# Eight sequences' states as moving operands in four column tiles, state eviction on VectorE, and a new order of steps, in a hybrid RWKV-7 / RetNet / MoE decoder step

## The reference, cut to what matters

```python
h = rmsnorm(x); proj = h @ w_in          # 2048 -> RWKV part (r,k,v,loras) and retention part (q,k,v,gate)
# RWKV-7, 16 heads x 64, per token, state S (value, key):
sa = S @ (-kk); S = S * w + outer(sa, b) + outer(v, k); y = S @ r
# then: group norm of y over the head, plus a bonus term, times a gate
# retention, 8 heads x 128, chunked, state R (key, value):
o = (q k^T * decay_in) v + (q R) * decay_q;   R = R * decay_c + (k * decay_k)^T v
x = x + concat(y_a, y_b) @ w_out
x = x + hier_moe(rmsnorm(x))             # top-1 of 4 groups, top-2 of 8 SwiGLU experts in it
y = rmsnorm(x)
```

## Time and profile before

| | us |
|---|---|
| median of 3 runs | 1986.51 (1985.43 to 1987.39) |
| the profiled execution's own time | 1987.42 |
| its span in the trace | 1985.3 |
| busy: TensorE (PE) | 1623.7, 82% |
| busy: VectorE (DVE) | 581.6, 29% |
| busy: ScalarE (ACT) | 288.5, 15% |
| busy: GpSimd (POOL) | 119.4, 6% |

### The profile page before, as it was taken

One profiled execution on the slowest core, in us unless ns is written; L12 is line 12 of the kernel. 1 busy time (PEld: TensorE's weight loads), 2 busy tenths in 40 slices (PEclk: granted clock), 3 DMA queues, 4 the chain that ended last, 5 costly groups with the idle time before them and its releaser, 6 DMA issues.

```text
span 1985.3 us, 25584 instructions
## 1 busy us (share of the span) xinstructions
PE 1623.7 (82%) x9086; PEld 1001.5 (50%) x9086; DVE 581.6 (29%) x1095; ACT 288.5 (15%) x577; POOL 119.4 (6%) x101
## 2 busy tenths in 40 slices
PE   8899999999999999999997668574867757676665
PEld 4677878686777777776774223132322312222111
DVE  6535454536354544431012111011110201111013
ACT  2222222222222222220012000000000000000002
POOL 1201111020202020200000000000000000000000
PEclk9999999999999999999999788787888878778778
DMA  7223222313223222217429999999999999999997
GB/s 287 81 79 115 78 99 74 111 67 108 84 77 112 77 102 87 95 63 281 181 117 385 428 427 428 428 429 429 428 428 428 428 429 428 429 429 428 428 409 261
DMA packets 71615, 510.34 MB, mean 257 GB/s; under 512 B 20464, under 2 KB 23664, under 8 KB 37648
## 3 DMA queue, kind: packets, MB, share of 16 engines
q1 hardware_dynamic: 71520, 509.60, 63.3%
q0 software_dynamic: 48, 0.12, 0.0%
HBM read 499.87 MB, written 9.82 MB: 257 GB/s over the span
## 4 chain that ended last, share of the span: by engine, by line
PE 54%; DMA 33%; DVE 7%; issue 2%; SPq 1%; ACT 1%; POOL 1%; DVEq 0%; POOLq 0%; ACTq 0%
DMA arena<-w_up 22%; PE ps_PJ L659 19%; DMA arena<-w_down 11%; PE ps_C L992 8%; DVE arena L1344 7%; PE ps_PJ L858 7%; PE ps_C L719 2%; PE ps_C L742 2%; SPq L515 1%; PE ps_C L1043 1%; PE ps_SB L1043 1%; PE ps_YB L1043 1%; PE ps_C L725 1%; PE ps_RT L824 1%; PE ps_SB L778 1%
## 5 line engine op out<-in xcount | busy, mean ns | idle before, releaser
L659 PE MATMUL ps_PJ<-arena 128*128 128x320 f32 x1792 | 536.6, 434 | 0.0
L992 PE MATMUL ps_C<-arena 128*32 128x512 f32 x2048 | 286.8, 723 | 189.6 <-DMA arena<-w_gate 113.1
L659 PEld LDWEIGHTS ps_PJ<-arena 128*128 128x128 f32 x1792 | 324.3, 191 | 112.3 <-issue 11.5
L992 PEld LDWEIGHTS ps_C<-arena 128*32 128x32 f32 x2048 | 79.5, 130 | 390.1 <-issue 387.7
L1344 DVE TENSOR_TENSOR arena<-arena,ps_PJ 128x512 f32<-128x512 f32 (+2 forms) x112 | 73.5, 657 | 614.9 <-PE ps_PJ L958 491.4
L1075 ACT ACTIVATE arena<-ps_C 128x512 f32<-128x512 f32 (+1 forms) x76 | 45.5, 598 | 1079.2 <-PE ps_C L992 581.4
L1344 DVE TENSOR_TENSOR arena<-arena 128x320 f32<-128x320 f32 (+13 forms) x254 | 143.8, 566 | 50.1 <-ACTq L379 25.8
L1832 POOL TENSOR_TENSOR arena<-arena 128x640 f32<-128x640 f32 (+2 forms) x80 | 113.6, 1420 | 734.2 <-ACTq L379 663.5
L858 PE MATMUL ps_PJ<-arena 128*128 128x320 f32 x512 | 144.1, 437 | 2.1 <-DVEq L379 2.1
L858 PEld LDWEIGHTS ps_PJ<-arena 128*128 128x128 f32 x512 | 96.5, 192 | 42.5 <-issue 6.2
L1075 ACT ACTIVATE arena<-arena 128x320 f32<-128x320 f32 (+11 forms) x149 | 79.6, 534 | 183.8 <-DVEq L379 60.6
(11 more groups left out here) (184 smaller groups left out, 1379.7 us busy)
## 6 DMA issues: line engine op xcount, KB each, us to landing
arena<-w_up SPq DMA_DIRECT2D x64, 2048.0 KB, 20.3
arena<-w_down SPq DMA_DIRECT2D x64, 2048.0 KB, 20.3
arena<-w_gate SPq DMA_DIRECT2D x60, 2048.0 KB, 21.0
arena<-win SPq DMA_DIRECT2D x59, 1024.0 KB, 4.8
arena<-w_out SPq DMA_DIRECT2D x16, 1024.0 KB, 5.8
arena<-w_gate SPq DMA_DIRECT2D x8, 1024.0 KB, 10.6
arena<-xT SPq DMA_DIRECT2D x8, 640.0 KB, 7.1
arena<-s_ret SPq DMA_DIRECT2D x8, 512.0 KB, 3.8
```

The costliest lines, as they stand in the source:

```text
L659: last = mm(pj(j)[:, 0:T], wt[j % NSLOT][:, kt, :], hT[:, kt, :], start=kt == 0, stop=kt == KT - 1)
L992: last = mm((GB, UB)[u][h * CAP:(h + 1) * CAP, :], xg[:, kt, h * CAP:(h + 1) * CAP], w[h][:, k, :], start=kt == 0, stop=kt == KT - 1)
```

## The change

Four things.

- In `sN` the product with the identity goes. VectorE takes the state out instead of ScalarE: `S = psum * w + Sw`, one fused operation, where `Sw` is the old state times the next decay, which VectorE makes right behind each eviction but the last (`s0` is a plain scaling).
- In `rs0` the operands change places. The 24 columns of a sequence are the stationary operand (`arx`, a copy with sequences outermost, made by ScalarE in step `pd`), the state is the moving one, 128 columns wide, and four sequences go to four column tiles of 32 output partitions, in two turns. The retention states that `oo` used one after another are done in the same way in `rs0` (`qdx` holds the 16-wide stationary operands, with zeros where another turn's sequence stands). The results lie as rows of sequences; they are put in order by products with 0/1 matrices: four products with 32-wide weights in `rs1`, one product in `oo`, two in `us`. `my` then copies all 320 columns of y at once.
- ScalarE's eviction of `rs0` is two copies (256 and 128 wide) for one of 192.
- The order: `ps` before `-s3`; `-mu` two fields later, behind `g4`; the five Gram products in four fields in a row, all of them in tile v; `lp ls` one field earlier; `v0 v1` ahead of `@v` on VectorE; `z1` stays in its field.

```diff
-    "r": "@k | -r3 | sq | -a3 ss | p1 | -s3 ps | | b1 b2a",
-    "v": "@r | | b2b | -my | -mu | g4 p2 | g0 | g1",
-    "q": "@v v0 g2 -va | g3 v1 | lp ls | | z1 | zs1 pd | | d1 ds1",
+    "r": "@k | -r3 | sq | -a3 ss | p1 | ps -s3 | | b1 b2a",
+    "v": "@r | | b2b | -my | g4 p2 | -mu g0 | g1 | g2 g3 v0",
+    "q": "v1 @v -va | lp ls | | | z1 | zs1 pd | | d1 ds1",
...
-                    if c > 0:
-                        mm(b[:, 0:P], ident, S, start=True, stop=False)
-                    mm(b[:, 0:P], tok[:, 1, c, :], SA, start=c == 0, stop=False)
+                    mm(b[:, 0:P], tok[:, 1, c, :], SA, start=True, stop=False)
...
-                    for i in range(NS):
-                        last = mm(ob[:, :, i * TS:(i + 1) * TS], S0[:, i, :], ar[:, :, i * TS:(i + 1) * TS], start=True, stop=True)
+                    for g in range(2):
+                        for c in range(4):
+                            mm(b[32 * c:32 * c + 24, g * P:(g + 1) * P], arx[:, 4 * g + c, :], S0[:, 4 * g + c, :], start=True, stop=True)
+                    for g in range(2):
+                        for c in range(4):
+                            last = mm(b[32 * c:32 * c + 16, 2 * P:3 * P], qdx[:, 4 * g + c, :], Rs0[:, 4 * g + c, :], start=g == 0, stop=g == 1)
...
-                    mm(b[:, 0:P], RTs[:, 0:P], ident, start=True, stop=False)
+                    for a in range(2):
+                        for g in range(2):
+                            mm(b[64 * a + 32 * g:64 * a + 32 * g + 32, 0:P], seq_heads[:, 32 * a:32 * a + 32], QA[:, g, :], start=True, stop=False)
...
+                    for g in range(2):
+                        mm(yb[:, 32 * g:32 * g + 32], QA[:, g, :], seq_rows[:, :, 16:24], start=False, stop=g == 1)
...
-                    for i in range(NS):
-                        cc = slice(TP + i * TS, TP + (i + 1) * TS)
-                        last = mm(b[:, cc], Rs0[:, i, :], qd[:, cc], start=False, stop=i == NS - 1)
-                    last.then_inc(full(s), 1)
+                    mm(b[:, TP:T], QO, seq_rows[:, :, 0:16].rearrange("p c (g t) -> p g c t", g=2), start=False, stop=True).then_inc(full(s), 1)
...
-                    A(S, bank(s)[:, 0:P], ACT.Copy, scale=wc(c)).then_inc(free(s), 1)
...
+                        TSC(S, bank(s)[:, 0:P], wc(0), None, ALU.mult).then_inc(free(s), 1)
+                    else:
+                        STT(S, bank(s)[:, 0:P], wc(c), Sw, ALU.mult, ALU.add).then_inc(free(s), 1)
+                    if c < NC - 1:
+                        TSC(Sw, S, wc(c + 1), None, ALU.mult)
```

More of the change, by code:

```diff
@@ L193, in build_program @@
         kdt, vrt = sb(384), sb(384)
+        qdx, seq_heads = qd[:, 0:P].rearrange("p (i n) -> p i n", i=NS), qd[:, TP:T]
+        arx = xm["k"][:, 0:24 * NS].rearrange("p (i n) -> p i n", i=NS)
         st = sb(T)
@@ L1140, in step @@
                     last.then_inc(done("vbd"), 1)
+                    wait_done(act, "bd", p)
+                    A(arx.rearrange("p i (a t) -> p a i t", a=3), AR[:, NC, :].rearrange("p (a i t) -> p a i t", a=3, i=NS), ACT.Copy).then_inc(done("arx"), 1)
                 elif s == "sq":
@@ L1183, in step @@
                     if s == "z5":
[L1184 to L1189, removed]
-                    A(S, bank(s)[:, 0:P], ACT.Copy, scale=wc(c)).then_inc(free(s), 1)
+                        A(wcs, e1[:, 0:TP].rearrange("p (c n) -> p c n", c=NC)[:, :, C - 1:C].rearrange("p c n -> p (c n)"), ACT.Copy).then_inc(done("wc"), 1)
                 elif s == "rs0":
                     wait_filled(act, s, p)
-                    A(RTs, bank(s)[:, 0:192], ACT.Copy).then_inc(free(s), 1)
+                    A(QA[:, :, :], bank(s)[:, 0:2 * P].rearrange("p (g n) -> p g n", g=2), ACT.Copy)
+                    A(QO, bank(s)[:, 2 * P:3 * P], ACT.Copy).then_inc(free(s), 1)
                 elif s == "va":
@@ L1422, in _ @@
                 shifted(lraw[j], lxm[j], lmu[0:m, j:j + 1], lmu[0:m, 3 + j:4 + j], m, sh_out[0:m, 24 + j, :], lora_xm)
+            for a in range(2):
+                CP(seq_heads[:, 32 * a:32 * a + 32].rearrange("p (c t) -> p c t", c=4), seq_rows[:, :, 8 * a:8 * a + 8])
             RED(sgn, rotm, AX_X, ALU.add)
@@ L1519, in step @@
                     CP(SA, bank(s)[:, 0:P]).then_inc(free(s), 1)
+                elif s in ("s0", "s1", "s2", "s3"):
+                    c = int(s[1])
+                    wait_filled(dve, s, p)
+                    if c == 0:
+                        wait_done(dve, "wc", p)
+                        if not first(p):
+                            dve.wait_ge(out_done["S"], 32 * p)
+                        TSC(S, bank(s)[:, 0:P], wc(0), None, ALU.mult).then_inc(free(s), 1)
[3 more added lines that the diff above has]
+                        TSC(Sw, S, wc(c + 1), None, ALU.mult)
                 elif s == "rs1":
@@ L1571, in step @@
                         dve.wait_ge(hc_in, 16 * (p + 1))
-                        TT(qd, x, dq, ALU.mult).then_inc(done("qrot"), 1)
+                        TT(qd[:, P:TP], x[:, P:TP], dq[:, P:TP], ALU.mult)
+                        for g in range(2):
+                            cc = slice(TP + 32 * g, TP + 32 * g + 32)
+                            last = TT(qdx[:, 4 * g:4 * g + 4, 8 * g:8 * g + 8], x[:, cc].rearrange("p (i t) -> p i t", i=4),
+                                      dq[:, cc].rearrange("p (i t) -> p i t", i=4), ALU.mult)
+                        last.then_inc(done("qrot"), 1)
                     else:
```

21 lines of the change are left out of this document (10 added, 11 removed), and 2 rows, old and new, of the table PLAN0.

## The result

The changed kernel takes 1958.28 us (median of 4 runs, 1957.59 to 1959.95) where the kernel before takes 1986.76 (median of 4, 1985.43 to 1987.39). The ratio is 0.9859, with a 95% interval of 0.9842 to 0.9876: 1.4% or 28.5 us less, a small gain, but clear of the noise. The profiled execution took 1959.95 (span 1958.2); that of before 1987.42 (span 1985.3).

What follows compares the result with a forecast made beforehand. TensorE bounds the mixing stage, busy 101.54 of 104.40 us a period. Loop 1.4 + 2.4 = 3.8 a pair, times 7, 26.6; first pair 1.2, tail +0.2: 27.6 less, 1986.51 to 1959 us, range 1953 to 1972.

Steps and rivals of the forecast that it cites:

- Work on TensorE: Per pair: 4.06 us of products removed, 2.68 added in `rs0`, `rs1`, `oo` and `us`; 1.4 us less.
- the round of four short passes: In `rs0`: four 128-column passes over four column tiles take 0.14 us a round, between 0.108 and 0.25.
- Rivals 1, 3 and 4: Column tiles dearer: loads not hidden, 1968 (13%); single file, 1982.5 (9%); single file with loads unhidden, 2017 (4%).
- rival 3: Short column-tile passes run in single file: 2.9 us a pair lost, 1982.5 us; chance 9%.
- rival 1: Weight loads in a column tile are not hidden: 0.25 us a round, 1968 us; chance 13%.
- The stretch from `s2` to `z1`: Holds all three TensorE waits; those at `lp` and `z1` go, `z1` starts 2.4 us earlier a pair.
- `ss` reaches VectorE 0.36 us earlier: In the `s2` to `z1` stretch: `a3`'s 0.29 wait goes, `s2` is 0.22 shorter; 575.54 instead of 575.90.
- Rival 2: The waits come back because VectorE sets the `s2` to `z1` stretch: 1.6 us a pair lost, 1970 us; chance 12%.
- rival 5: The gain is taken back by unseen waits: 1986 us; chance 3%.
- "I expect no clock effect there": In the mixing stage the granted clock is 1.00 (2.4 GHz), even where TensorE waits; no effect expected.
- First pair, tail, expert stage: Written-out first pair gains 1.2 us; behind the loop `s1` costs 0.65, `s2` and `s3` give 0.44: +0.2.
- "The expert stage keeps its length": Expert stage: DMA engines busy throughout at 428 GB/s, untouched by the change, so mixing-stage gains reach the end in full.

Runs made afterwards that it cites:

- one_tile: Changed kernel with all short products of `rs0` in the first column tile instead of four (output not the reference's): 1979.86 us.
- order_only: Kernel before with the new order table alone; state evictions on ScalarE and identity products stay: 1966.08 us, ratio 0.9896.
- evict_only: Kernel before with VectorE's fused state eviction alone, without identity products, old order but for `ps` ahead of `s3`: 1996.14 us, ratio 1.0039.
- tiles_only: Kernel before with the column tiles alone; old order, ScalarE evicts the states, identity products stay: 1973.58 us, ratio 0.9939.
- no_evict: Changed kernel with column tiles and new order, but states evicted on ScalarE and added by the identity as before: 1957.73 us, ratio 0.9854.
- same_tile_first: Changed kernel with loops exchanged for `rs0` and the retention states, so four passes in a row go to one tile: 1958.91 us, ratio 0.9847.
- g4_late: Changed kernel with one table row altered: `g4` and the `p2` behind it one part of a projection later: 1952.09 us, ratio 0.9823.
- s3_late_g4_late: Changed kernel with `g4` one part of a projection later and VectorE's eviction of `s3` behind the copy of y: 1947.6 us, ratio 0.9792.
- no_evict_g4_late: Changed kernel with the old state eviction on ScalarE and `g4` one part of a projection later: 1950.71 us, ratio 0.9813.
- old_order_filled: Changed kernel under the whole old order, with six 320-column matmuls added ahead of the wait at `mu`: 1987.28 us, ratio 1.0006.

## Why the prediction was right, and what in it was off

The forecast was 27.6 us less; the profiled execution gave 27.5 and the medians 28.5. The forecast 3.8 a pair is the measured 3.80. That agreement is partly luck: two terms were off in opposite directions.

1. **Work on TensorE**, forecast -1.4 a pair, measured about -1.6. The removed 4.06 is gone in full. Of the added 2.68, `rs1` came to 0.60 (0.35 for its tiles, 0.20 more on the product behind, 0.05 on the next projection) for 0.62, `us` to 0.42 for 0.43, `oo` to 0.22 for 0.17, but `rs0` to 1.20 (0.57 + 0.44 + 0.19) for 1.46. The term that was mis-sized is the round of four short passes: I took 0.14, between 0.108 and 0.25, and it is 0.11, the lower end. Entering the mode costs about 0.13 (0.57 less 0.44), leaving it 0.19 to 0.2.
2. **Rivals 1, 3 and 4** fall with that number. `one_tile` shows what rival 3 would have looked like: 3.6 us in `rs0`, which with its order and eviction still ends at 1980. The Trainium skill's rule that a weight load overlaps a running matmul only when the row group differs (TensorE: Matmul & The Clock Gate, The mechanism), on which rival 1 leant, does not describe these rows: four tiles with the same rows took 0.11 us a round, and even one tile 0.110 to 0.117 a pass. The kernel before could have said so: eight full-width passes of a projection, all with the same rows, take 2.16 us (the first line shown under 3), or 0.27 each, while their eight weight loads take 1.92 us beside them.
3. **The stretch from `s2` to `z1`**, forecast -2.4, measured about -2.2 (from `s2`'s first product to `z1`'s start it is 2.0 shorter, and `z1` itself, without a wait ahead, 0.27). The step that failed in it is that `ss` reaches VectorE 0.36 us earlier, for which the prediction names two terms, 0.29 and 0.22, and no sum. Measured from `s2`'s first product (568.88 before and 551.80 now, in the chains), k's shift did begin earlier, 2.44 us behind it for 3.23 (572.11), 0.8 instead of the 1.3 I wrote. But the wait at `a3` that this was to remove had cost next to nothing. It is a wait of the weight load alone, and the chain of before shows the products in a row across it:

```profile
572.82 2.16 PE ps_PJ L659 x8
574.98 0.27 PE ps_C L755 x2
```

   There `a3` takes 0.27 instead of its usual 0.22, so its wait was worth 0.05. The identity gave 0.22, and of that `s2`'s first product took back 0.15 (its weight load sits idle for 0.40 us first); the product of `ss` is 0.07 shorter (0.56 for 0.63). Together `ss` reached VectorE 0.19 earlier. The eviction of `s3` with its idle time cost VectorE's chain 0.59 instead of 0.43. `g4` therefore started 0.56 earlier than `mu` had, not 0.96, and waited 1.5, not 1.3. From `g4` to `z1` it is 13.73 us for the forecast 13.7, without a wait. That is the half of the mechanism that carries the gain, and `order_only` has it nearly alone: 2.67 us a period.
4. **Who brings what.** In the new order the parts nearly add: 104.38 to 101.71 by the order, to 100.38 by the tiles, to 100.58 by VectorE's eviction. My forecast put the eviction down as a gain (earlier k) with a price (`s3`); shown is that it costs 0.2 a period as built.
5. **Rival 2** (the waits come back) did not come true, nor did rival 5 (1986 us), but its ground was good: VectorE's chain did grow, and under the old order its growth, with the low clock that follows the longer wait, turns the whole change into a loss of 7 us.
6. **The clock.** "I expect no clock effect there" held for this change; I had taken it from the row of before. What I had not seen is what longer waits do: in the loops the waits of 1.7 us and less were never followed by a low clock, those of 2.4 in five of seven periods, those of 3.5 in all seven. A forecast from the waits alone is then too low by 1.5 to 1.7 us a period.
7. **First pair, tail, expert stage.** Up to the first `rs0` the gain is 0.33 us and from the last one on 1.54, together 1.9 where I had 1.2 less 0.2; that 0.9 and the 1.4 that the expert stage lost (below) nearly cancel, which is luck too. Behind the loop I had `s1` on VectorE at 0.65 and gains of 0.44. The wait at `r` (L758) grew from 0.47 to 1.36:

```profile
848.29 0.46 PE L758 MATMUL ps_C<-arena 128*128 128x128 f32 x2 [1.36 <-DVEq L382]
```

`evict_only` has the same 1.36 and `tiles_only` the old 0.5, so it is the eviction's, 0.89 for my 0.65. "The expert stage keeps its length" was wrong for the profiled execution by 1.4 us. Two windows near its end, of the changed kernel first (the last products), then the same place in the kernel before:

```profile
1936.00:1940.00 4.00, 3.17 (x17) 0.57 (x17) 0.00 (x0) 0.60 (x1) 0.00 (x0) 0.69 0.00 0
```

```profile
1964.00:1968.00 4.00, 2.94 (x19) 0.96 (x20) 0.00 (x0) 0.60 (x1) 0.00 (x0) 1.00 0.00 0
```

The last products came at a granted clock of 0.69 instead of 1.00. Some 910 us into the stage its steps are 0.2 us behind those of before, at 920 us 1.4, so the lost 1.4 us are there (earlier in the stage they drift apart by up to 3 us and come together again). `no_evict` (stage 939.7), `same_tile_first` (940.0) and `g4_late` (941.1) have it too; the other nine kernels profiled have 937.2 to 937.7, and two of them (`s3_late_g4_late`, `no_evict_g4_late`) start the stage earlier than any other. It goes with the execution, then, not with how early the stage starts. In twelve of the thirteen kernels a wait of 2.8 to 3.1 us for a transfer stands ahead of these products, and in four of them the clock is low behind it; what decides it is open. It would explain why the profiled execution is the slowest of its four, and the 1.0 us between the 27.5 and the 28.5 above.

8. **A low clock behind the loop.** The longest wait of TensorE behind the loop, at the transposes (L880, L885 in the changed kernel), is 2.8 us before, 2.3 in the changed kernel, 0.6 in `order_only` and 0.7 in `tiles_only`, with the same code. The rows say why. A wait of 2.12 us stands a little ahead of it, with eight passes of a projection between the two. First the kernel before, then `order_only`:

```profile
895.52 2.39 PE L858 MATMUL ps_PJ<-arena 128*128 128x320 f32 x8 [2.12 <-DVEq L379]
900.68 0.68 PE L880 MATMUL ps_C<-arena 128*128 128x128 f32 x3 [2.77 <-DVEq L379]
...
876.27 4.08 PE L858 MATMUL ps_PJ<-arena 128*128 128x320 f32 x8 [2.12 <-DVEq L379]
880.94 0.55 PE L880 MATMUL ps_C<-arena 128*128 128x128 f32 x3 [0.59 <-DVEq L379]
```

and the windows of some 4 us behind the second wait before, and behind the first in `order_only`:

```profile
900.65:904.65 4.00, 3.96 (x11) 2.71 (x12) 0.49 (x1) 0.00 (x0) 0.00 (x0) 0.57 1.09 355
...
876.25:880.35 4.10, 4.08 (x8) 2.19 (x8) 1.14 (x4) 0.00 (x0) 0.00 (x0) 0.58 0.82 252
```

In `order_only` the low clock comes behind the first wait, stretches the eight passes from 2.39 to 4.08 us and is paid out of the second wait, whose end TensorE does not set. In the kernel before it comes behind the second wait, where nothing hides it. The five kernels with a low clock between the two waits (`order_only`, `tiles_only`, `old_order_filled`, `no_evict`, `no_evict_g4_late`) have 0.6 to 1.2 us at the transposes, the other eight 2.3 to 2.8. From the end of that wait to the expert stage it is 147.25 us in the changed kernel, with the low clock, and 145.55 in `same_tile_first`, which has none there. So 1.7 us of a total hang on where, and whether, the low clock falls; that is most of the 2.2 us by which `order_only` came out lower than seven of its periods make it. A difference of less than 2 us between two totals here may be this alone; the periods of the kernels whose waits in the loop are 1.7 us or shorter don't hold it.

## What to carry to other kernels

When short matmuls have narrow stationary operands, four column tiles take them four at a time at the price of one stream a round (0.11 us instead of four times that here), and the visit costs about 0.3 us on top; by these figures it is even after one round and pays from the second. An edit that moves work from the bounding engine to another is worth its saved time only if the other engine's chain does not end the next wait: read that wait's releaser first, and move the work behind it, as the late eviction of `s3` did. And a wait on TensorE can have a second price, a low clock behind it: look at the granted clock behind each wait, and keep the wait short or fill it before making another engine's chain longer. When a low clock falls just ahead of another wait, it costs nothing, so compare kernels by their periods as well as by their totals.

## What the hardware showed that I had not expected

- In the loop a wait of 2.4 us on TensorE was followed in five of seven periods by some 3 us at half the granted clock, at a cost of 1.5 to 1.7 us on top of the wait, and one of 3.5 us in seven of seven. Filling that longer wait with 3.2 us of products whose result nobody reads made the period 1.57 us shorter.
- The length of a wait did not settle it: behind the loop a wait of 2.12 us was followed by the low clock in five of 13 kernels, and a second one, of 2.3 to 2.8 us, in six of the other eight, with the same code.
- Four column tiles with passes of 128 columns: 0.11 us a round, whatever the order in which the tiles are addressed, with about 0.13 us to enter and 0.19 to leave. The same passes in one tile: 0.110 to 0.117 each, their weight loads hidden.
- The last products of the kernel met the low clock in the profiled executions of four kernels and not in those of the other nine, for 1.4 to 3.7 us of the span.
